# Mixture-of-experts weights read in 8192-byte runs, and results spread by an exact one-hot matrix in one-pass products

## What is computed

```python
h = rmsnorm(x)                                  # gain ffn_norm_g
# top-1 of 4 groups, then top-2 of its 8 experts -> eid, gate (2 per token)
args: xb = rows of one expert, e = its number
y = (silu(xb @ w_gate[e]) * (xb @ w_up[e])) @ w_down[e]     # 2048 -> 512 -> 2048
out = segment_sum(y * slot_gate[:, None], slot_tok)         # back to the tokens
x = x + out
```

## Time and profile before

| | |
|---|---|
| median of 3 runs | 1909.73 us (1907.47 to 1911.05) |
| span of the profiled execution | 1907.9 us |
| PE busy | 1736.2 us, 91% of the span |
| DVE, ACT, POOL busy | 669.3, 290.6, 174.4 us |
| read from HBM | 484.28 MB |
| queue of SP | 470.84 MB, its packets 67.1% of 16 engines' span |

### The profile page before, as it was taken

How to read it: one execution, slowest core, us unless ns; L and a number is a source line. 1 busy time by engine, 2 the same in 40 slices (tenths; PEclk the granted TensorE clock), 3 DMA queues, 4 the chain that set the end, 5 groups by cost and what they waited for, 6 DMA issues and landing times.

```text
span 1907.9 us, 20510 instructions
## 1 busy us (share of the span) xinstructions
PE 1736.2 (91%) x7715; PEld 927.1 (49%) x7715; DVE 669.3 (35%) x982; ACT 290.6 (15%) x546; POOL 174.4 (9%) x255
## 2 busy tenths in 40 slices
PE   7979999999999869858999999898899889999998
PEld 6567788868886454823333333333333333333332
DVE  1467766554434232430332133132222303312233
ACT  3122344342221122200000000000000000000000
POOL 0181053410000000110000000000000000000000
PEclk9989999999999979769999999999999999999999
DMA  7213322162325200439999999999999999999994
GB/s 280 75 45 88 88 67 64 48 204 89 108 90 199 88 1 5 172 127 390 386 392 387 390 394 381 396 378 390 376 382 393 375 392 384 391 384 386 392 392 187
DMA packets 213256, 484.39 MB, mean 254 GB/s; under 512 B 9458, under 2 KB 47452, under 8 KB 192988
## 3 DMA queue, kind: packets, MB, share of 16 engines
q1 hardware_dynamic: 209168, 470.84, 67.1%
q0 software_dynamic: 3456, 12.88, 2.3%
q10 hardware_dynamic: 588, 0.07, 0.0%
HBM read 484.28 MB, written 8.39 MB: 258 GB/s over the span
## 4 chain that ended last, share of the span: by engine, by line
PE 76%; DMA 15%; DVE 4%; issue 2%; ACT 2%; SPq 1%; ACTq 0%; POOL 0%; DVEq 0%; POOLq 0%
PE ps L1661 14%; DMA weight_ring<-in_expert_w_up_dram 14%; PE ps L1639 13%; PE ps L1372 10%; PE ps L1690 10%; PE ps L1486 9%; PE ps L1569 3%; PE ps L1505 3%; PE ps L1317 2%; PE ps L1621 2%; PE ps L1332 1%; PE ps L1345 1%; SPq L427 1%; PE ps L1578 1%; PE ps L1406 1%
## 5 line engine op out<-in xcount | busy, mean ns | idle before, releaser
L1661 PE MATMUL ps<-weight_ring,transposed_acts 128*64 128x512 f32 x2048 | 472.2, 597 | 56.5 <-DMA weight_ring<-in_expert_w_up_dram 55.6
L1661 PEld LDWEIGHTS ps<-weight_ring,transposed_acts 128*64 128x64 f32 x2048 | 153.1, 137 | 369.6 <-issue 271.6
L1690 PE MATMUL ps<-weight_ring,transposed_acts 128*64 128x512 f32 x1024 | 230.2, 602 | 18.3 <-issue 16.2
L1639 PE MATMUL ps<-proj_buffer 128*128 128x512 f32 x512 | 245.1, 615 | 1.4 <-DVE proj_buffer L1278 1.4
L1259 DVE TENSOR_TENSOR residual<-ps,residual 128x512 f32<-128x512 f32 x256 | 177.0, 691 | 61.9 <-PE ps L1639 61.6
L1690 PEld LDWEIGHTS ps<-weight_ring,transposed_acts 128*64 128x64 f32 x1024 | 72.6, 138 | 163.1 <-issue 160.5
L1639 PEld LDWEIGHTS ps<-proj_buffer 128*128 128x128 f32 x512 | 78.7, 188 | 145.6 <-DVE residual L1259 132.2
L1249 DVE TENSOR_TENSOR transposed_acts<-ps,gains_T 128x512 f32<-128x512 f32 x66 | 42.5, 685 | 285.0 <-PE ps L1621 284.9
L1372 PE MATMUL ps<-mix_high,w_in_high 128*128 128x512 f32 x288 | 117.9, 409 | 9.3 <-DVE w_in_low L932 9.3
L1372 PE MATMUL ps<-mix_high,w_in_low 128*128 128x512 f32 x288 | 113.3, 393 | 0.0
L1372 PE MATMUL ps<-normed_low,w_in_high 128*128 128x512 f32 x288 | 113.2, 393 | 0.0
(11 more groups left out here) (251 smaller groups left out, 1790.8 us busy)
## 6 DMA issues: line engine op xcount, KB each, us to landing
weight_ring<-in_expert_w_gate_dram SPq DMA_DIRECT2D x128, 1024.0 KB, 15.7
weight_ring<-in_expert_w_up_dram SPq DMA_DIRECT2D x128, 1024.0 KB, 15.2
weight_ring<-in_expert_w_down_dram SPq DMA_DIRECT2D x128, 1024.0 KB, 14.3
weight_ring<-in_w_in_dram SPq DMA_DIRECT2D x18, 1024.0 KB, 5.7
weight_ring<-in_w_out_dram SPq DMA_DIRECT2D x16, 1024.0 KB, 5.1
weight_ring<-in_xkv_w_dram SPq DMA_DIRECT2D x8, 1024.0 KB, 6.2
residual<-in_x_dram SPq DMA_DIRECT2D x8, 1024.0 KB, 18.7
weight_ring<-in_xq_w_dram SPq DMA_DIRECT2D x4, 1024.0 KB, 5.1
```

The source lines that it names most:

```text
L1639: mm(ps[:, 6 + i % 2, :], spread[:, t * P:(t + 1) * P], y[:, n, :], start=True, stop=True).then_inc(part_done, 1)
L1661: ins = mm(ps[side * SLOTS:(side + 1) * SLOTS, 0, :], xsT[:, par, k, :], w[:, kk, :], start=(k == 0), stop=(k == KD - 1), skip_group_check ...
L1690: ins = mm(ps[half, 4 + n // 2, :], act_t[:, f * SLOTS:(f + 1) * SLOTS], w[:, n * 512:(n + 1) * 512], start=(f == 0), stop=(f == KF - 1), ...
```

## The change

1. Gate and up are read so that partition p gets the rows 16p to 16p+15, and a chunk holds four rows one after another: 8192 bytes in one piece, in place of four pieces of 2048 bytes. A chunk's pieces lie 32 KiB apart. Down is read as before, with the access written flat.
2. For the rows of the product to fit, L807 writes `hs` in the order (k, p) from the order (p, k) of `X`, that is with a step of 16 elements in what it reads, and the gain is loaded a second time in that order (`gF`, one more DMA of ACT).
3. `spread` becomes a one-hot matrix without the gate, in the one-pass type F32R. ACT writes the down result times the gate to `y_hi` in F32R, in two activations (one a half), and DVE writes what that rounding lost to `y_lo`, in two `scalar_tensor_tensor`, each behind its activation. The two take the place of one activation and one copy.
4. Each of the 16 products becomes two: `spread` x `y_hi` and `spread` x `y_lo`, added up in PSUM.

```diff
-        gate_v = expert_w_gate[0].rearrange("e (k p) n -> e p k n", p=P)
+        gate_v = expert_w_gate[0].rearrange("e (p c k) n -> e p c (k n)", c=4, k=4)
...
-                return (gate_v, up_v)[j % 2][ds(e, 1), :, 4 * (j // 2):4 * (j // 2) + 4, :].rearrange(
-                    "e p k n -> p (e k) n")
+                return (gate_v, up_v)[j % 2][ds(e, 1), :, j // 2, :].rearrange("e p m -> p (e m)")
...
+            act.dma_start(gF[:, :], ffn_norm_g[0].rearrange("(p k) -> p k", k=KD)).then_inc(small_in, 16)
...
-                a.activation(hs[:, t % 2, :], X[:, t, :], ACT.Copy, scale=stat[:, 2, 10 + t:11 + t]).then_inc(rows_ready, 1)
+                a.activation(hs[:, t % 2, :].rearrange("q (k p) -> q k p", p=P),
+                             X[:, t, :].rearrange("q (p k) -> q k p", k=KD), ACT.Copy,
+                             scale=stat[:, 2, 10 + t:11 + t]).then_inc(rows_ready, 1)
...
-                a.activation(y[par * SLOTS:(par + 1) * SLOTS, 0:4:2, :], ps[0:SLOTS, 4:6, :], ACT.Copy).then_inc(y_act, 1)
+                for side in range(2):
+                    rows = slice(side * SLOTS, (side + 1) * SLOTS)
+                    a.activation(y_hi[par * SLOTS:(par + 1) * SLOTS, side:4:2, :], ps[rows, 4:6, :], ACT.Copy,
+                                 scale=gate[rows, ds(b, 1)]).then_inc(y_act, 1)
...
-                    v.tensor_scalar(spread, tramp, tokf[:, ds(b - 1, 1)], gate[:, ds(b - 1, 1)],
-                                    ALU.is_equal, ALU.mult).then_inc(spread_ready, 1)
-                dve.wait_ge(used, b * 12 + (UE + 12))
-                v.tensor_copy(y[par * SLOTS:(par + 1) * SLOTS, 1:4:2, :], ps[SLOTS:2 * SLOTS, 4:6, :]).then_inc(y_dve, 1)
+                    v.tensor_scalar(spread[:, :], tramp, tokf[:, ds(b - 1, 1)], None, ALU.is_equal).then_inc(spread_ready, 1)
+                for side in range(2):
+                    rows = slice(side * SLOTS, (side + 1) * SLOTS)
+                    dve.wait_ge(y_act, b * 2 + (side + 1))
+                    v.scalar_tensor_tensor(out=y_lo[par * SLOTS:(par + 1) * SLOTS, side:4:2, :], in0=ps[rows, 4:6, :],
+                                           scalar=gate[rows, ds(b, 1)],
+                                           in1=y_hi[par * SLOTS:(par + 1) * SLOTS, side:4:2, :].bitcast(F32),
+                                           op0=ALU.mult, op1=ALU.subtract).then_inc(y_dve, 1)
...
-                    mm(ps[:, 6 + i % 2, :], spread[:, t * P:(t + 1) * P], y[:, n, :],
-                       start=True, stop=True).then_inc(part_done, 1)
+                    mm(ps[:, 6 + i % 2, :], spread[:, t * P:(t + 1) * P], y_hi[:, n, :],
+                       start=True, stop=False)
+                    mm(ps[:, 6 + i % 2, :], spread[:, t * P:(t + 1) * P], y_lo[:, n, :],
+                       start=False, stop=True).then_inc(part_done, 1)
```

More of the change, by code:

```diff
@@ L90, in hybrid_block @@
             pass
+        with ExitStack() as shared:
+            shared.enter_context(nc.sbuf_tensor("below_y_low", [P, 4096], F32))
+            y_lo = shared.enter_context(nc.sbuf_tensor("y_low", [P, 4, 512], F32R))
         H = sb("transposed_acts", [P, KD, S])
+        with ExitStack() as shared:
+            shared.enter_context(nc.sbuf_tensor("below_y", [P, 2 * D], F32))
+            y_hi = shared.enter_context(nc.sbuf_tensor("y_high", [P, 4, 512], F32R))
+            spread = shared.enter_context(nc.sbuf_tensor("spread", [P, S], F32R))
         PB = sb("proj_buffer", [P, NCT * S])
@@ L99, in hybrid_block @@
         gT = sb("gains_T", [P, NGR])
+        gF = sb("ffn_gain_by_row", [P, KD])
         stat = sb("norm_stats", [P, 3, 14])
@@ L411, in _ @@
                     for j in range(8):
-                        sp.dma_start(slot(expert_slot(j)).rearrange("p (k n) -> p k n", n=FF),
-                                     expert_chunk(0, j)).then_inc(landed[expert_slot(j)], 16)
+                        sp.dma_start(slot(expert_slot(j)), expert_chunk(0, j)).then_inc(landed[expert_slot(j)], 16)
                 last = [m for m in range(n) if early[m][0] == s]
@@ L420, in _ @@
                 sp.wait_ge(o_done, 28)
-                sp.dma_start(slot(s).rearrange("p (k n) -> p k n", n=D), expert_chunk(0, j)).then_inc(landed[s], 16)
+                sp.dma_start(slot(s), expert_chunk(0, j)).then_inc(landed[s], 16)
             def load_expert(e, b):
@@ L426, in load_expert @@
                     sp.wait_ge(used, b * 12 + (UE - 12 + j + 1))
-                    sp.dma_start(slot(s).rearrange("p (k n) -> p k n", n=FF if j < 8 else D),
-                                 expert_chunk(e, j)).then_inc(landed[s], 16)
+                    sp.dma_start(slot(s), expert_chunk(e, j)).then_inc(landed[s], 16)
             with sp.Fori(1, NE) as b:
@@ L997, in _ @@
                     dve.wait_ge(bias_built, 2)
-                    dve.wait_ge(small_in, 48)
+                    dve.wait_ge(small_in, 64)
                 if i == 2:
@@ L1234, in _ @@
             link(v.tensor_copy(gate[0:SLOTS, :], r["fin"][0:SLOTS, TCOL:2 * TCOL]))
-            link(v.tensor_copy(gate[SLOTS:P, 0:TCOL - 1], r["fin"][0:SLOTS, TCOL + 1:2 * TCOL]))
+            link(v.tensor_copy(gate[SLOTS:P, :], r["fin"][0:SLOTS, TCOL:2 * TCOL]))
             zero = r["one"][0:SLOTS, 0, :]
@@ L1638, in spread_parts @@
                             pe.wait_ge(part_added, before + (i - 1))
-                    mm(ps[:, 6 + i % 2, :], spread[:, t * P:(t + 1) * P], y[:, n, :],
-                       start=True, stop=True).then_inc(part_done, 1)
+                    mm(ps[:, 6 + i % 2, :], spread[:, t * P:(t + 1) * P], y_hi[:, n, :],
+                       start=True, stop=False)
+                    mm(ps[:, 6 + i % 2, :], spread[:, t * P:(t + 1) * P], y_lo[:, n, :],
+                       start=False, stop=True).then_inc(part_done, 1)
             def last_pair(blocks):
-                pe.wait_ge(y_act, blocks)
-                pe.wait_ge(y_dve, blocks)
+                pe.wait_ge(y_dve, 2 * blocks)
                 pe.wait_ge(spread_ready, blocks // 2)
@@ L1667, in block_pe @@
                 if behind:
-                    pe.wait_ge(y_act, b)
-                    pe.wait_ge(y_dve, b)
+                    pe.wait_ge(y_dve, b * 2)
                     pe.wait_ge(spread_ready, pair)
@@ L1681, in block_pe @@
                 pe.wait_ge(act_ready, b + 1)
-                wait_past(pe, y_act, b)
-                wait_past(pe, y_dve, b)
+                wait_past(pe, y_dve, b * 2)
                 for f in range(KF):
```

8 lines of the change are left out of this document (3 added, 5 removed).

## The result

| | before | after |
|---|---|---|
| median of 4 runs each, on one chip | 1908.66 us (1907.47 to 1911.05) | 1858.57 us (1857.78 to 1859.04) |
| ratio | | 0.9739 [0.9728, 0.9751] |
| span of the profiled execution | 1907.9 us | 1856.6 us |
| first expert's gate and up start | 836.62 | 835.37 |
| last even block's turn starts | 1838.90 | 1790.13 |

The change takes 50.1 us off the median and 51.3 us off the profiled span. 1855.4 us was forecast. The last three rows divide the span in two: the stretch that waits for weights went from 1002.3 to 954.8 us (−47.5), the tail behind the last wait from 69.0 to 66.5 us (−2.5). The other 1.3 us lie before the first expert; in the executions profiled here this start lies between 832.6 and 837.2 us, so I count them for nothing.

What follows compares the result with a forecast made beforehand. The DMA weight stream was taken to set the pace until 1835.2 us, then PE the end; −50.7 − 6.4 + 2.4 + 0.4 = −54.3 us makes 1907.9 into 1853.6, plus 1.8 for the median: 1855.4 us, range 1840 to 1885.

Steps and rivals of the forecast that it cites:

- The term of −50.7 us: Gate and up stream: runs of 8192 bytes reach down's 418.5 GB/s in place of 386, 601.3 us against 652.0.
- the residue left for a gather: Weight stream, 844 to 1835.2 us: 48.6 us left over for 31 gathers, 1.57 us each.
- A pair of 63.2 us: Expert stream: a pair of blocks falls from 66.6 to 63.2 us, PE's work 61.1 at most, the stream still the bound.
- The products: 16 products a pair: 3.2 us less PE time, worth nothing in the stream, counted twice behind the last wait, −6.4 us.
- y in two parts: After the down product: about 3.7 us to the last `y_dve` against 1.33, uncovered only before the last pair, +2.4 us.
- Rival E: PE becomes the bound, by a lower clock with shorter products or a round trip that doesn't shrink: 1870 us, chance 0.03.
- the clock is 1.00 in the stream: PE's granted clock in the weight stream: 1.00 in spite of 2.5 us waits, said against the rival of PE as bound.
- The strided reads of `hs`: Normed rows read with a step of 16 elements: 1.99 to 4 us each, covered by 36 us of POOL's wait, 0 us.
- One more DMA on ACT: At the start, ahead of the first square sum: an issue of 0.45 us, +0.4 us (0 to 0.6).
- B: Gate and up stream: run length is only part of the gap between 386 and 419; 400 GB/s, 1883 us, chance 0.14.
- C: Gate and up stream: the 32 KiB pitch makes it slower; at 347 GB/s 1979 us in all, chance 0.07.
- D: Gate and up transfers are still cut into 2048-byte pieces; only the tail's −3.6 is left, 1906 us, chance 0.03.

Runs made afterwards that it cites:

- E1: The kernel before with only the gate and up reads changed (with `gF` and strided `hs`), old products, `y` and `spread`: 1861.88 us, ratio 0.9762.
- E3: The kernel after with gate and up runs of 8192 bytes placed 8 KiB apart in place of 32 KiB: 1858.47 us, ratio 0.9747.
- E4: The kernel after, each partition keeping its 16 rows, but a chunk taking every fourth, so runs of 2048 bytes: 1906.32 us, ratio 0.9998.
- E5: The kernel after with two groups of eight rows a partition, so gate and up runs of 4096 bytes: 1872.38 us, ratio 0.9810.
- E6: The kernel after with gathers of 512 bytes for each filled slot in place of 8192, from the first 256 KiB of `normed_rows`: 1801.95 us, ratio 0.9442.
- E2: The kernel before with old reads but the new products, `y` in two parts and the one-hot matrix: 1902.02 us, ratio 0.9973.
- E8: The kernel after, last pair starting on the first side of `y`, with 12 small products of ones keeping PE at work before it: 1856.35 us, ratio 0.9728.
- E11: The kernel after with 16 small products of ones ahead of the last pair and its order unchanged: 1857.36 us, ratio 0.9736.

## Why the prediction was right, point by point

- **The stream is the bound, and the length of the run sets its rate.** Shown by E1 (the reads alone take off 45.6 us, 1907.48 to 1861.88), E3, E4 and E5. The term of −50.7 us came out at −47.5 because two errors nearly cancel. The new rate was 421, not 418.5: gate and up take 251.7 / 421 = 597.9 us, 54.1 less than 652.0, and down gains 1.8 more. But the residue left for a gather is 1.80 us, not 1.57, 7.1 us for 31. −54.1 − 1.8 + 7.1 is −48.8, the difference of the two windows (991.2 to 942.4), of which 1.25 is the earlier start of the first expert. The gather's price is a residue in both kernels, and E6 bears it out for the kernel after alone. That it grew is not shown: with 388 GB/s for gate and up, the other window of the earlier trace rows, the kernel before's is 1.67 us already. That the errors nearly cancel was luck; the range had room for either (2.0 us a gather, +13).
- **A pair of 63.2 us** was 63.41, and the wait for up chunks stayed. E1, where it fell to 40.9 us, shows that the shorter products keep PE away from the bound, as forecast.
- **The products are worth nothing in the stream and count in the tail.** Shown by E1 and E2. Two adds start 1.51 us apart at the full clock, as worked out. Behind the last even block the stretch from the turn to the odd block's gate and up shrank from 23.69 us (1838.90 to 1862.59) to 20.34 (1790.13 to 1810.47), −3.35 for the −3.2 of the sum.
- **y in two parts**: 4.04 us from PE's last down product to the first product, against 1.33, so +2.7 for +2.4. The activation took 1.11 us and the two-input operation 1.28 to 1.30, as the 1.02 and 1.23 with up to 0.1 more each for the gate. These three make 3.7 of the 4.04 us; the other 0.3 are the hand-overs from PE to ACT to DVE to PE, which the sum left out.
- **The step that was missed** is in the last pair's products: −3.2 was forecast, −1.9 came (16.04 to 14.15 us from first product to last add), since the clock fell in the stop. Rival E had a lower clock in it, by shorter products and in the stream; what lowered it here was the longer empty stop, which no gate and up work covers. E8 and E11 show it. The tail gave 2.5 us in all where 4.0 was forecast: 0.3 of the miss is in y, 1.3 in these products. The prediction's "the clock is 1.00 in the stream" holds for its windows, not all over: the kernel before has 0.50 from 1414.3 to 1417.6 us and again from 1748.8 to 1752.2.
- **The strided reads of `hs`** take 3.79 us each, near the bound of 4, and stay hidden. POOL's memset behind them starts at 789.6, and POOL still waits 34.15 us for the router's table:

```profile
789.59 3.51 POOL L552 MEMSET proj_buffer<- 128x4096 f32 x1 [5.66 <-DMA normed_rows<-proj_buffer]
...
827.25 0.56 POOL L560 IOTA proj_buffer<- 128x512 f32 x1 [34.15 <-DVE proj_buffer L1252]
```

- **One more DMA on ACT**: its issue took 0.45 us, and what stands behind it on ACT moved by 0.48. That it reaches the end of the kernel, as the +0.4 of the sum has it, no run shows: the first expert starts 1.25 us earlier in the kernel after, and at 836.59 in E1, which has the same issue, where the kernel before has 836.62.

Of the rivals, B would have shown windows of 400, C below 386, D the same number of packets, E no waits for up chunks; the page and the windows after exclude each.

What stays open: why E2's median fell by 2 us more than its tail shows, what slows the packets of a gather to 64 partitions, and what the 0.1 to 0.2 us are that one over 128 costs beyond its bytes.

## What to carry to other kernels

Where a full stream is the bound, compare windows of the same kernel in which only one kind of transfer is in flight. Where two rates stand at the same DMA share, compare the lengths of the runs first; here they were the whole difference, and the better rate was the gain at hand. Then look for what dips in it: here a small transfer to half of the partitions cost nearly three times its bytes' time (1.8 us against 0.62). A forecast for a rewritten operation holds in the stream by its cover, and has to be made again for the last round, where there is none and where a longer stop may lower PE's clock for what comes next.

## What the runs showed of the hardware

- A read from HBM in a full stream moved 386 to 388 GB/s in runs of 2048 bytes, 408 to 410 in 4096 and 419 to 422 in 8192, at a DMA share of 1.01 to 1.05 each; a packet took 88, 164 and 313 ns. Pitches of 8 and 32 KiB gave the same.
- A gather of 0.26 MB to the first 64 partitions cost the stream 1.7 to 1.8 us, its packets of 8192 bytes taking 455 ns in the median where the weights' take 313; the same bytes over 128 partitions cost about 0.8 us.
- PE's clock fell to 1.2 GHz in an empty stop of 4.04 us and came back 5 us after the products had begun; a stop of 2.73 us, two parts and one of 0.94 us also lowered it, for some 3 us. 12 to 16 small products in the stop kept it at 1.00. In the kernel after's stream, with single waits of up to 2.9 us, one window of 10 us in 94 shows less than 1.00, and that fall stands behind 1.9 us of turns and a stop of 1.07 us, not behind a wait for weights.
- An ACT copy of 128 x 2048 float32 took 3.79 us where the read steps by 16 elements, and 1.99 where it doesn't.
